# The last down-projection of a two-block layer, turned so that the tokens lie on the partitions

## What is computed

```python
h = h + rmsnorm(mixed, norm_mix_post_w[layer])
f = rmsnorm(h, norm_ffn_pre_w[layer])
f = jnp.square(jax.nn.relu(f @ w_up[layer])) @ w_down[layer]
h = h + rmsnorm(f, norm_ffn_post_w[layer])
```

## Time and profile before

| what | value |
|---|---|
| timed runs, us | 1285.31, 1284.50, 1283.51 |
| median, us | 1284.5 |
| the profiled execution, us | 1283.23 |
| its span, first to last instruction, us | 1281.1 |
| mean granted TensorE clock | 0.988 |
| TensorE busy, us (matmuls) | 1234.9 |
| VectorE busy, us | 799.1 |
| ScalarE busy, us | 659.4 |
| DMA moved, MB | 210.27 |

### The profile page before, as it was taken

How to read it: one execution, slowest core, us unless ns; L and a number is a source line. 1 busy time by engine, 2 the same in 40 slices (tenths; PEclk the granted TensorE clock), 3 DMA queues, 4 the chain that set the end, 5 groups by cost and what they waited for, 6 DMA issues and landing times. The chain is left out here.

```text
span 1281.1 us, 22409 instructions
## 1 busy us (share of the span) xinstructions
PE 1234.9 (96%) x9900; PEld 1209.5 (94%) x9900; DVE 799.1 (62%) x866; ACT 659.4 (51%) x764; POOL 10.5 (1%) x23
## 2 busy tenths in 40 slices
PE   7999999999999999999989999899899998999996
PEld 6999999999999999999989989898899997999996
DVE  6655666777664557774456567787874554777442
ACT  6443444677543445553344468777864444455330
POOL 0000000000000000000000000000000000000000
PEclk9999999999999999999999999999999998999998
DMA  8553454454665545556545555455356552556540
GB/s 290 165 164 100 136 161 140 141 172 141 198 197 174 188 132 169 193 178 217 189 141 183 157 149 165 148 165 152 128 182 197 186 177 66 171 192 212 183 132 33
DMA packets 210240, 210.27 MB, mean 164 GB/s; under 512 B 6476, under 2 KB 207564, under 8 KB 210144
## 3 DMA queue, kind: packets, MB, share of 16 engines
q1 hardware_dynamic: 207600, 200.30, 49.2%
q0 software_dynamic: 1968, 7.64, 2.1%
q10 hardware_dynamic: 576, 0.90, 0.2%
HBM read 207.73 MB, written 1.09 MB: 163 GB/s over the span
## 5 line engine op out<-in xcount | busy, mean ns | idle before, releaser
L236 PE MATMUL ps<-x_hi,w_hi 128*128 128x256 f32 x2752 | 792.1, 288 | 12.2 <-DVE x_lo L1120 8.7
L236 PE MATMUL ps<-x_lo,w_hi 128*128 128x256 f32 x2752 | 781.5, 284 | 0.0
L236 PE MATMUL ps<-x_hi,w_lo 128*128 128x256 f32 x2752 | 781.3, 284 | 0.0
L204 DVE TENSOR_TENSOR w_lo<-raw,w_hi 128x2048 fp32r<-128x2048 f32 x188 | 429.9, 2290 | 252.1 <-ACT w_hi L198 252.1
L236 PEld LDWEIGHTS ps<-x_hi,w_hi 128*128 128x128 f32 x2752 | 530.8, 193 | 18.7 <-issue 13.6
L236 PEld LDWEIGHTS ps<-x_lo,w_hi 128*128 128x128 f32 x2752 | 531.2, 193 | 0.9
L236 PEld LDWEIGHTS ps<-x_hi,w_lo 128*128 128x128 f32 x2752 | 530.8, 193 | 0.0
L198 ACT CAST w_hi<-raw 128x2048 fp32r<-128x2048 f32 x188 | 355.2, 1899 | 117.6 <-PE ps L236 115.4
L1364 PE MATMUL ps<-arena,cst 128*128 128x256 f32 (+1 forms) x240 | 57.7, 380 | 19.4 <-ACT arena L767 12.2
L236 PE MATMUL ps<-w_hi,x_hi 128*128 128x256 f32 x240 | 69.1, 288 | 2.4 <-DVE w_lo L204 2.4
L1364 PE MATMUL ps<-arena 128*128 128x256 f32 (+3 forms) x448 | 68.3, 341 | 2.3 <-ACT arena L747 2.3
(11 more groups left out here) (174 smaller groups left out, 685.6 us busy)
## 6 DMA issues: line engine op xcount, KB each, us to landing
raw<-in_w_in SPq DMA_DIRECT2D x170, 512.0 KB, 4.7
raw<-in_w_ff SPq DMA_DIRECT2D x64, 512.0 KB, 4.5
raw<-in_w_up SPq DMA_DIRECT2D x32, 512.0 KB, 4.7
raw<-in_w_down SPq DMA_DIRECT2D x32, 512.0 KB, 4.4
raw<-in_w_mem_kv SPq DMA_DIRECT2D x16, 512.0 KB, 5.0
raw<-in_w_out SPq DMA_DIRECT2D x16, 512.0 KB, 4.9
raw<-in_w_ssm_proj SPq DMA_DIRECT2D x16, 512.0 KB, 4.7
raw<-in_w_x_proj SPq DMA_DIRECT2D x8, 512.0 KB, 4.8
```

Source lines behind the costliest of these rows:

```text
L204: nc.vector.tensor_tensor(w_lo[:, s], raw[:, s], w_hi[:, s].bitcast(FP32), ALU.subtract)\
L236: last = nc.tensor.matmul(dst, l, r, start=start and k == 0 and m == 0, stop=stop and k == nk - 1 and m == 2)
```

## The change

In the second down-projection the operands swap sides: the activation tile is stationary and the weights stream, so each PSUM bank holds 128 tokens by 256 output features (`deep(..., TOK)`). The norm over the features is then a sum along the free axis. ScalarE squares each bank with a row sum (`final_square`), VectorE multiplies it by the gain (`final_out`), which is loaded once as a row broadcast to all partitions (`y_g`, on the POOL queue). The two engines take the two banks of a column in opposite order. The partial sum of the first three columns becomes the bias of the Ln; after the last column two Ln and two Exp over one column give the factors, and VectorE makes four operations of 128x512 that scale and add the residual.

The residual has to be turned for that. This is done during the up-projection: behind its units 2 to 5 TensorE transposes four tiles of `res` each into bank 7, and ScalarE copies the bank to `y_res` in the steps 3 to 6 of `hidden` (`turned`). The output goes out in four DMAs of 256 KB, one behind each of the four last operations. The former end is gone. The semaphores that count the high and low parts of the branch outputs in five other stages (`c_hi`, `s_hi`, `m_hi`, `a_hi`, `d_hi` and the same with `lo`) are merged into two, `y_hi` and `y_lo`, with running counts; those lines are left out below.

```diff
@@ SP
-            sp.wait_ge(S("y_ready"), 4)
-            sp.dma_start(out[0].rearrange("(t p) d -> p t d", p=P), cells(0, 2, D)).then_inc(S("y_out"), 16)
-            sp.wait_ge(S("y_out"), 16)
+            for b in range(4):
+                t, v = b // 2, y_cols(b % 2, 512)
+                sp.wait_ge(S("y_ready"), b + 1)
+                sp.dma_start(out[0, t * P:(t + 1) * P, v], y_f[:, t, v]).then_inc(S("y_out"), 16)
+            sp.wait_ge(S("y_out"), 64)
@@ POOL
+            pool.wait_ge(S("r_post"), 4)
+            pool.dma_start(y_g, a["norm_ffn_post_w_2"][0].partition_broadcast(P)).then_inc(S("y_g"), 16)
@@ ScalarE
+            def turned(c):
+
+                if 3 <= c < 7:
+                    g = c - 3
+                    act.wait_ge(S("r_ct"), g + 1)
+                    A(y_res[:, g // 2, y_cols(g % 2, 512)], bank(7, 512), ACT.Copy).then_inc(S("r_turned"), 1)
+
+            def hidden(stage, c0, extra=None):
...
                     A(f, unit_bank(u), ACT.Relu).then_inc(taken(u), 1)
                     split()
+                    if extra is not None:
+                        extra(c)
                     act.wait_ge(S("f_sq"), c + c0 + 1)
...
-            hidden("up2", 16)
-            deep(mix, 2, 14)
-            inverse(4)
-            for b in range(2):
-                act.wait_ge(S("end_t"), 2 * b + 2)
-                A(cells(0, 2, D)[:, 1, 512 * b:512 * b + 512], bank(5 + b, 512), ACT.Copy).then_inc(S("y_ready"), 1)
+            hidden("up2", 16, turned)
+
+            def final_square(c, t):
+
+                if t == 0:
+                    finished(act, U("down2", 4 * c + 3))
+                else:
+                    act.wait_ge(S("y_f1"), c + 1)
+                A(y_sq[2 * c + t], y_bank(c, t), ACT.Square, accum_out=y_ss[:, t, c:c + 1]).then_inc(S("y_sq"), 1)
+
+            for b in range(16):
+                if b < 14:
+                    split()
+                if b % 4 == 3 and b < 15:
+                    for t in range(2):
+                        final_square(b // 4, t)
+            act.wait_ge(S("y_bias"), 1)
+            for t in range(2):
+                final_square(3, t)
+                act.wait_ge(S("y_sq"), 7 + t)
+                chain(A(y_rs[:, t:t + 1], y_ss[:, t, 3:4], ACT.Ln, bias=y_bias[:, t:t + 1], scale=1.0 / D))
+                A(y_rs[:, t:t + 1], y_rs[:, t:t + 1], ACT.Exp, scale=-0.5).then_inc(S("y_rs"), 1)
@@ VectorE
-            deep("down2", mix, False, 14)
-            scaled(4, mix, 0)
...
+            def final_out(c):
+
+                v = y_cols(c)
+                if c == 0:
+                    dve.wait_ge(S("y_g"), 16)
+                finished(dve, U("down2", 4 * c + 3))
+                tt(y_f[:, 1, v], y_bank(c, 1), y_g[:, v], ALU.mult).then_inc(S("y_f1"), 1)
+                dve.wait_ge(S("y_sq"), 2 * c + 1)
+                tt(y_f[:, 0, v], y_bank(c, 0), y_g[:, v], ALU.mult).then_inc(S(f"deep{c % 2}"), 1)
+
+            for b in range(16):
+                if b < 14:
+                    split()
+                if b == 13:
+                    dve.wait_ge(S("y_sq"), 6)
+                    chain(V.tensor_reduce(y_bias, y_ss[:, :, 0:3], AXX, ALU.add))
+                    ts(y_bias, y_bias, 1.0 / D, EPS, ALU.mult, ALU.add).then_inc(S("y_bias"), 1)
+                if b % 4 == 3:
+                    final_out(b // 4)
+            dve.wait_ge(S("deep1"), 5)
+            dve.wait_ge(S("r_turned"), 4)
+            for t in range(2):
+                dve.wait_ge(S("y_rs"), t + 1)
+                for h in range(2):
+                    v = y_cols(h, 512)
+                    stt(y_f[:, t, v], y_f[:, t, v], y_rs[:, t:t + 1], y_res[:, t, v], ALU.mult, ALU.add)\
+                        .then_inc(S("y_ready"), 1)
@@ TensorE
-            def deep(stage, done0):
+            def deep(stage, done0, tok=FP):
...
                     if b % 4 == 0:
                         pe.wait_ge(S(f"deep{c % 2}"), c // 2 + done0 + 1)
+                        if tok and c > 1:
+                            pe.wait_ge(S("y_sq"), 2 * (c - 2) + 2)
...
             for i in range(1, 16):
                 unit(U("up2", i), H0)
-            deep("down2", 2)
-            for b in range(4):
-                norm(4, b)
-
-            for b in range(2):
-                pe.wait_ge(S("end"), 2 * b + 2)
-                for t in range(2):
+                if 2 <= i < 6:
+                    g = i - 2
+                    pe.wait_ge(S("r_post"), 4)
+                    pe.wait_ge(S("n_r"), 4)
+                    need(pe, "r_turned", g)
                     for k in range(4):
-                        last = tr(bank(3 + 2 * t + b, 4, P)[:, k], res[:, 4 * b + k, t * P:(t + 1) * P])
-                    last.then_inc(S("end_t"), 1)
+                        last = tr(bank(7, 4, P)[:, k], res[:, 4 * (g % 2) + k, g // 2 * P:(g // 2 + 1) * P])
+                    last.then_inc(S("r_ct"), 1)
+            deep("down2", 2, TOK)
```

More of the change, by code:

```diff
@@ L271, in build, with y_bank, y_cols @@
                                                   cells(2576, 2, T), cells(3088, T), cells(7056, 2, T))
+        y_f, y_g, y_res = cells(0, 2, D), cells(2048, D), cells(4400, 2, D)
+        y_sq = [cells(n, T) for n in (3072, 3328, 3584, 3840, 6448, 6704, 6960, 7216)]
+        y_ss = small[:, 210:218].rearrange("p (t c) -> p t c", t=2)
+        y_bias, y_rs = small[:, 218:220], small[:, 220:222]
+        def y_bank(c, t):
+            return bank(3 + c % 2 * 2 + t, T)
+        def y_cols(c, n=CW):
+            return slice(c * n, (c + 1) * n)
         def rs_row():
@@ L485, in cross @@
                 act.wait_ge(S("c_y"), j + 1)
-                A(rows(x_hi, 2 * j + YX, 2), bank(6, 2, T), ACT.Copy).then_inc(S("c_hi"), 1)
+                A(rows(x_hi, 2 * j + YX, 2), bank(6, 2, T), ACT.Copy).then_inc(S("y_hi"), 1)
                 if i < 4:
@@ L511, in stick_out @@
                 act.wait_ge(S("s_y"), j + 1)
-                A(rows(x_hi, 2 * j + YSB, 2), bank(7, 2, T), ACT.Copy).then_inc(S("s_hi"), 1)
+                A(rows(x_hi, 2 * j + YSB, 2), bank(7, 2, T), ACT.Copy).then_inc(S("y_hi"), 1)
             for i in range(1, 4):
@@ L566, in mlstm_out @@
                 act.wait_ge(S("m_y"), j + 1)
-                A(rows(x_hi, 2 * j + YML, 2), m_hm, ACT.Copy).then_inc(S("m_hi"), 1)
+                A(rows(x_hi, 2 * j + YML, 2), m_hm, ACT.Copy).then_inc(S("y_hi"), 1)
             split()
@@ L719, in att_out @@
                 act.wait_ge(S("a_y"), j + 1)
-                A(rows(x_hi, 2 * j + YAT, 2), bank(7, 2, T), ACT.Copy).then_inc(S("a_hi"), 1)
+                A(rows(x_hi, 2 * j + YAT, 2), bank(7, 2, T), ACT.Copy).then_inc(S("y_hi"), 1)
             split()
@@ L776, in ssm_out @@
                 act.wait_ge(S("d_yn"), j + 1)
-                A(rows(x_hi, 2 * j + YSS, 2), d_y, ACT.Copy).then_inc(S("d_hi"), 1)
+                A(rows(x_hi, 2 * j + YSS, 2), d_y, ACT.Copy).then_inc(S("y_hi"), 1)
             att_exps(2)
@@ L962, in cross @@
                 split()
-                low(2 * j + YX, bank(6, 2, T), "c_hi", j + 1, "c_lo")
+                low(2 * j + YX, bank(6, 2, T), "y_hi", j + 1, "y_lo")
                 if i == 4:
@@ L1002, in _ @@
                 split()
-                low(2 * (i - 1) + YSB, bank(7, 2, T), "s_hi", i, "s_lo")
+                low(2 * (i - 1) + YSB, bank(7, 2, T), "y_hi", i + 4, "y_lo")
             def conv(pad, dst, name, tiles, stride):
@@ L1055, in mlstm_gate @@
                 tt(m_hm, m_hm, m_o, ALU.mult).then_inc(S("m_y"), 1)
-                low(2 * j + YML, m_hm, "m_hi", j + 1, "m_lo")
+                low(2 * j + YML, m_hm, "y_hi", j + 9, "y_lo")
             split()
@@ L1066, in _ @@
             split()
-            low(6 + YSB, bank(7, 2, T), "s_hi", 4, "s_lo")
+            low(6 + YSB, bank(7, 2, T), "y_hi", 8, "y_lo")
             mlstm_conv(0)
@@ L1226, in att_low @@
             def att_low(j):
-                low(2 * j + YAT, bank(7, 2, T), "a_hi", j + 1, "a_lo")
+                low(2 * j + YAT, bank(7, 2, T), "y_hi", j + 13, "y_lo")
             split()
@@ L1260, in ssm_skip @@
             def ssm_skip(j):
-                need(dve, "d_lo", j)
+                if j:
+                    dve.wait_ge(S("y_lo"), j + 15)
                 for c in range(2):
@@ L1287, in ssm_low @@
             def ssm_low(j):
-                low(2 * j + YSS, d_y, "d_hi", j + 1, "d_lo")
+                low(2 * j + YSS, d_y, "y_hi", j + 16, "y_lo")
             att_logits(2)
```

26 lines of the change are left out of this document (9 added, 17 removed).

## The result

The kernel after takes 1290.06 us (median of 5 runs, 1289.25 to 1290.68) against 1284.5 us: ratio 1.0046, 95% interval 1.0035 to 1.0057. That is 5.6 us more, where 4.9 us more were forecast (1289.4 us). Its profiled execution took 1290.39 us with a span of 1288.6 us.

What follows compares the result with a forecast made beforehand. TensorE, full from 1085 us, and the 17.3 us tail were taken to decide the time; -11.0 + 2.0 + 9.4 + 4.5 = +4.9 us on 1284.5 gave 1289.4 us, range 1284.3 to 1293.0.

Steps and rivals of the forecast that it cites:

- tail: From the last product to the span's end: 6.3 us instead of 17.3, so 11.0 us less (9.2 to 11.7).
- transposes: 16 on a full TensorE in the up-projection, 0.5 us a group of four: 2.0 us more (1.5 to 4).
- three waits: Up-projection: TensorE stops for ScalarE's copy of bank 7, 3.13 us each, 9.4 us more (8.5 to 10.5).
- clock behind them: Up-projection: clock falls to half after all three pauses, 3.4 us long, 1.5 us each: 4.5 us more (0 to 7.8).
- T: End of the last product, from which the tail was counted; the last VectorE operation was to end at T+3.6.
- the rival that four writes would hinder each other: Tail: the last write lands 4.5 us behind its issue instead of 2.7; +6.7 us in all, 1291.2 us; 5%.
- The first rival: Up-projection: clock holds in all pauses (+0.4, 1284.9 us) or all but one (1286.4 us); 20%.
- The third rival: Up-projection: TensorE doesn't meet the wait, pauses and falls vanish; -9.0 us, 1275.5 us; 5%.
- What costs nothing: Swapped down-projection sides, ScalarE's copies, work on finished banks, the gain's broadcast and merged semaphores were to add no time.
- the second rival: Up-projection: low clock lasts longer because transposes follow the pause; +8.2 us, 1292.7 us; 15%.

Runs made afterwards that it cites:

- e1: The kernel after with the four transpose groups behind units 2, 4, 6 and 8 and ScalarE's copies in steps 3, 5, 7 and 9; 1274.04 us, ratio to before 0.9923.
- e3: The kernel after without the residual's transposes, their waits and ScalarE's four copies, adding untransposed rows (output not the reference's); 1273.04 us, ratio to before 0.9913.
- e4: The kernel after with 24 unread products more on TensorE ahead of each of the three waits; 1285.23 us, ratio to before 1.0001.
- e8: The kernel after with ScalarE's copy of bank 7 at the end of its step, behind the write-back of the high part; 1291.76 us, ratio to before 1.0052.
- e9: The same kernel as e1, timed again beside e10 and e11; 1275.53 us, ratio to before 0.9929.
- e6: e1 with ten unread fp32 matmuls more on TensorE between the third norm and the up-projection; 1274.87 us, ratio to before 0.9922.
- e10: The same kernel as e7, timed again beside e9; 1273.27 us, ratio to before 0.9915.
- e11: The same kernel as e5, timed again beside e9; 1276.33 us, ratio to before 0.9940.
- e2: The kernel after with ScalarE's copy of bank 7 ahead of the split of its step instead of behind it; 1279.9 us, ratio to before 0.9967.
- e5: e1 with one output write of 1024 KB instead of four of 256 KB; 1277.75 us, ratio to before 0.9943.
- e7: e6 with added matmuls also in the other pauses of 2 us and more of the second block; 1273.01 us, ratio to before 0.9912.

## Why the prediction was right, and where it was off

The forecast was 4.9 us more, the result 5.6. Term by term, from the stages of the table above:

| term | forecast | measured | from |
|---|---|---|---|
| tail | -11.0 | -10.7 | 17.28 to 6.55 |
| transposes | +2.0 | +1.7 | e1 against e3 |
| three waits | +9.4 | +9.6 | e4 against e1 |
| clock behind them | +4.5 | +5.7 | after against e4 |
| sum | +4.9 | +6.3 | |

That the result came within 0.7 us of the forecast is in part luck: the terms of the traces sum to 1.4 us more than was forecast, and another 1.2 us lie ahead of the stage. The spans of the two profiled executions are 7.5 us apart, the medians 5.6, because before's execution lay 1.3 us under its median and after's 0.3 us above.

- **The tail** was read rightly in its parts, with two small errors of opposite sign. VectorE's last operation ends at T + 3.99 us and not T + 3.6: the four scale-and-add operations take 0.69 us each from start to start (2.74 for four), not 0.60, and the first starts at T + 1.25 (ScalarE's Ln over one column takes 0.29 us, not 0.18). The last write takes 2.56 us to the end, where 2.7 were taken; the rival that four writes would hinder each other has no ground.
- **The transposes**: 0.44 us a group, 1.73 us for 16, so 0.11 us for each of these fp32 transposes in a full stream. The Trainium skill, page "TensorE: Matmul & The Clock Gate", section "Part 4: PE-mode transpose", has about 275 ns for one. The trace agrees with it as the duration of one, 272 ns (e1). The prediction's estimate of 1.1 us a group, 4.4 us for 16, took this duration for the distance from one to the next; that reading was wrong, and not the figure.
- **The waits** came out as the order of the two programs said: three, none behind unit 2, each Relu, split and copy, 3.19 us of delay instead of 3.13.
- **The clock** fell behind all three, as forecast. Its price is the term that was mis-sized: two falls of 3.4 us at 1.5 each would be 3.0, but the second lasted 6.8 us, and the three together cost 5.7. In the trace of before the prediction counted nine pauses of over 2 us, of which three left the clock up; there are ten and four (22.00, 851.46, 874.72 and 898.27 us), which changes none of its terms. With pauses of 3 us a long fall was one in three, in after as in e8; the prediction had it as a rival for all three or none.
- **The first rival**, the clock held, was priced at 1284.9 us; made true in e4, it is 1285.23 us. It didn't come about by itself. The Trainium skill's section "Why this matters for your kernels" on the same page warns of pauses above some 3 us between bursts. By the trace the pauses were 3.06 us in after, just above it, so this case agrees with the rule there; but the falls behind pauses of 2.1 us in the earlier trace rows don't.
- **The third rival**, in which TensorE never waits, was priced at 1275.5 us; made true in e1, it is 1274.04 and, timed again (e9), 1275.53 us.
- **What costs nothing** held: the down-projection is as fast in the new form (e3), and VectorE's and ScalarE's work on its banks never made TensorE wait. That the time came back entirely when only the distance between groups changed (e1) leaves no room for the merged semaphores or the broadcast of the gain; the stages with the merged semaphores lie ahead of 1085 us, and e1 begins its stage 0.17 us behind before.

One thing stays open: whether the transposes behind the pause lengthen the fall, as the second rival supposed. After and e8 have one long fall in three, but no run put products in the place of the transposes.

## What to carry to other kernels

When a step is moved from an idle tail into a stage that one engine fills, its work is the small price (here 1.7 us against 10.7 gained); look for the signal that comes back. A wait on an engine that runs in step with the waiting one costs nothing if the signal was given one unit earlier, and everything that stands ahead of it in the other engine's step if it was not, so give a buffer that is used again at least one unit of distance, or two buffers. And before paying to keep TensorE's clock up, see what a fall costs at its place: here one of 3.4 us cost 1.5 us, 0.8 us or nothing.

## What the runs showed of the hardware that was not expected

**Pauses of about 2 us cost the clock in one execution and not in another.** Between 10 and 35 us all these kernels run the same instructions, with a pause of about 2.5 us that ends at 22 us. In the traces of before, after, e1, e4, e6, e8, e10 and e11 the clock stayed up there; in those of e2, e3, e5, e7 and e9 it fell. The table of stretches, e1 first, then e9, the same kernel:

```profile
10.00:35.00 25.00, 22.50 (x171) 21.55 (x171) 19.47 (x29) 15.63 (x21) 0.00 (x0) 1.00 0.80 263
```

```profile
10.00:35.00 25.00, 22.55 (x163) 21.84 (x162) 18.61 (x28) 15.65 (x20) 0.00 (x0) 0.93 0.79 261
```

The five in which it fell come to the product behind the pause at 21.47 to 21.59 us, the eight others at 21.88 to 22.98; no run was made to move that moment. Of e1 and e9, at 668 us e9 is 0.70 us behind (667.69, 668.39); the stage starts at 1085.25 us in the one and at 1087.44 in the other, the rest coming from later falls, which don't lie at the same places either. Of the kernels with unfilled pauses those without that fall start it at 1085.0 to 1086.6, those with it at 1087.2 to 1087.6. Such differences ahead of the stage can account for spans and timed medians of these kernels that disagree by 1 to 2 us (for the timed runs that isn't shown), and because of them the lengths of the stage, which agree to 0.01 us between executions of one kernel (180.48 in e1, e5, e6, e7, e9 and e10), were the better measure of terms of this size.

Longer pauses were not certain either. The pause of 2.89 us that ends at 668 us stands in eleven traces (e7 and e10 have it filled); the clock fell behind it in ten and stayed up in e8, where the product behind it starts at 668.61 us. One of 2.60 to 2.62 us at 935 to 939 us left it up in e2, e3, e5, e7 and e9 and brought it down in e10. The pauses of 3.06 and 3.58 us in after and e8 brought it down six times in six, those of 1.27 us in e2 in none of three.

**The same fall has several prices.** Behind after's three pauses the falls of 3.4, 6.8 and 3.4 us cost 5.7 us; from 660 to 1060 us, taking away four falls brought the next stage forward by 1.3 us (e10 against e1, with one fall in e10 that e1 hasn't) and by 3.3 us (e7 against e9).
